# Rank columns beside the cross-attention queries, and the first up-projection begun in the output phases

## The reference

```python
for i in range(2):
    h = rms_norm(x, mix_norm[i])
    tok, xq = gla_mixer(h, ...) if i == 0 else dilated_mixer(h, ...)
    xa = memory_cross_attention(xq, mem_n, xa_w_kv[i], ...)
    x = x + concatenate([tok, xa]) @ w_out
    x = x + conv_ffn(rms_norm(x, ffn_norm[i]), w_up, conv_w, conv_b, w_down)
# gla_mixer: q, k, v, glr, og, xq = split_cols(h @ w_in, [384, 384, 768, 16, 768, 256])
#   log_a = log_sigmoid(glr @ w_gate2 + b_gate) / 16; chunked_gla(q, k, v, log_a); rms_norm(o) * silu(og)
# conv_ffn: u = causal_dwconv(h @ w_up, conv_w, conv_b); gate, val = split(u); (silu(gate) * val) @ w_down
```

## Time and profile before

| | us |
|---|---|
| median of 3 runs (2761.82 to 2763.5) | 2762.37 |
| the profiled execution | 2763.15 |
| its span (first to last instruction) | 2761.4 |
| PE busy | 2632.4 |
| PEld busy | 2224.0 |
| DVE busy | 1323.3 |
| ACT busy | 862.5 |
| POOL busy | 190.9 |

### The profile page before, as it was taken

How to read it: one execution, slowest core, us unless ns; L and a number is a source line. 1 busy time by engine, 2 the same in 40 slices (tenths; PEclk the granted TensorE clock), 3 DMA queues, 4 the chain that set the end, 5 groups by cost and what they waited for, 6 DMA issues and landing times. The chain is left out here.

```text
span 2761.4 us, 33638 instructions
## 1 busy us (share of the span) xinstructions
PE 2632.4 (95%) x12612; PEld 2224.0 (81%) x12612; DVE 1323.3 (48%) x2372; ACT 862.5 (31%) x1802; POOL 190.9 (7%) x265
## 2 busy tenths in 40 slices
PE   7998989989999999998999999998889999999999
PEld 7995767868888888886888888787768888888887
DVE  4422445435454455447463572453645445445445
ACT  6424434322222222224334433334332222222221
POOL 1000012000000000001211021111000000000000
PEclk9998999999999999999999999999899999999999
DMA  4211002122111111111101101102412111111111
GB/s 143 92 54 28 19 27 77 46 59 63 49 50 49 46 52 47 46 46 70 61 31 69 36 31 46 48 30 81 150 63 61 47 46 46 59 48 50 49 38 61
DMA packets 159282, 152.81 MB, mean 55 GB/s; under 512 B 27593, under 2 KB 129721, under 8 KB 159161
## 3 DMA queue, kind: packets, MB, share of 16 engines
q1 hardware_dynamic: 155000, 151.20, 17.1%
q10 hardware_dynamic: 4160, 0.02, 0.1%
HBM read 134.37 MB, written 16.83 MB: 55 GB/s over the span
## 5 line engine op out<-in xcount | busy, mean ns | idle before, releaser
L359 PE MATMUL psum<-hT_hi,f_up_hi 128*128 128x512 f32 x1408 | 435.8, 391 | 14.7 <-DVE f_up_lo L240 14.7
L359 PE MATMUL psum<-hT_lo,f_up_hi 128*128 128x512 f32 x1408 | 435.3, 390 | 0.0
L359 PE MATMUL psum<-hT_hi,f_up_lo 128*128 128x512 f32 x1408 | 434.8, 390 | 0.0
L50 PE MATMUL psum<-w_hi,hT_hi 128*128 128x512 f32 (+2 forms) x960 | 355.0, 370 | 19.5 <-DVE w_lo L736 11.3
L240 DVE TENSOR_TENSOR f_up_lo<-raw,f_up_hi 128x1024 fp32r<-128x1024 f32 x88 | 107.6, 1225 | 506.2 <-ACT f_up_hi L182 506.2
L52 PE MATMUL psum<-w_hi,hT_lo 128*128 128x512 f32 (+2 forms) x960 | 349.8, 364 | 0.0
L51 PE MATMUL psum<-w_lo,hT_hi 128*128 128x512 f32 (+2 forms) x960 | 349.6, 364 | 0.0
L359 PEld LDWEIGHTS psum<-hT_hi,f_up_hi 128*128 128x128 f32 x1408 | 265.1, 189 | 70.5 <-DVE f_up_lo L240 15.5
L359 PEld LDWEIGHTS psum<-hT_lo,f_up_hi 128*128 128x128 f32 x1408 | 265.4, 188 | 55.4
L359 PEld LDWEIGHTS psum<-hT_hi,f_up_lo 128*128 128x128 f32 x1408 | 265.3, 188 | 55.4
L182 ACT ACTIVATE f_up_hi<-raw 128x1024 fp32r<-128x1024 f32 x88 | 93.1, 1060 | 634.2 <-PE psum L359 599.8
(11 more groups left out here) (260 smaller groups left out, 3636.6 us busy)
## 6 DMA issues: line engine op xcount, KB each, us to landing
raw<-in_ffn_w_up_dram SPq DMA_DIRECT2D x88, 512.0 KB, 3.8
f_down_raw<-in_ffn_w_down_dram SPq DMA_DIRECT2D x22, 1024.0 KB, 4.8
w_raw<-in_b_w_in_dram SPq DMA_DIRECT2D x18, 1024.0 KB, 5.6
w_raw<-in_a_w_in_dram SPq DMA_DIRECT2D x8, 768.0 KB, 5.5
group_out<-stage SPq DMA_DIRECT2D x24, 256.0 KB, 2.3
o_outs<-group_out SPq DMA_DIRECT2D x24, 256.0 KB, 3.4
XY<-in_x_dram SPq DMA_DIRECT2D x8, 512.0 KB, 10.4
w_raw<-in_xa_w_kv_dram SPq DMA_DIRECT2D x8, 512.0 KB, 3.6
```

Of the source, the lines that this page charges most:

```text
L50: nc.tensor.matmul(out, lhs_hi, rhs_hi, start=start, stop=False)
L359: mm = nc.tensor.matmul(psum[:, 2 * j + half, :], w[j][:, d, :], h[:, d, half * HALF:(half + 1) * HALF], start=first, stop=final)
```

## The change

1. The rank columns are no longer loaded by the guest and projected in the gated phase. The block of the cross-attention queries gets them as 16 further columns (`beside_w`): SP loads them with a transfer of their own behind each half of the weights, the split and the matmuls cover 272 columns for 256, and ACT copies them out of PSUM per tile into `rank_rows`. The block now stands ahead of the two gate blocks, so that the second gate block ends the phase. In the gated phase eight turns of 128 x 16 (`turn_rank`) bring the rank columns into rows; `high(0)`, `low(0)` and `project(0, 0)` are gone, and the semaphore counts shift by one.
2. The split buffers of the up-projection (`FirstUp`) are made before the output phase and kept into the feed-forward phase; `y_hi`, `y_lo` use them until they are free. In the last tile the output phase makes the split of units 0 and 1, and PE does the first half (512 tokens) of each (`up_half`) behind the last output matmuls and behind the last turns. The turns of tile 6, and its gain and split, move ahead of the second half of tile 7. The feed-forward phase does only the second half of these two units, and its waits for `up_split` count from unit 2; SP's loads of units 2 and 3 wait for nothing there.
3. The stage tiles of the second layer are placed from the other side of the memory.

The diff, cut to its core:

```diff
# ffn_phase
                         n = g * 4 + 2 * c + j
                         if is_first(g) and c == 0:
                             continue
-                        sp.wait_ge(up_split, n - 1)
+                        if not is_first(g):
+                            sp.wait_ge(up_split, n - 3)
                         raws.load(sp, j, up_unit(w_up, j, g * 2 + c))
...
-                sp.wait_ge(up_split, 2 * FC)
+                sp.wait_ge(up_split, 2 * FC - 2)
...
-            high_up(0, 0)
-            high_up(1, 1)
             act.wait_ge(taps_ready, 1)
...
-            low_up(0, 0)
-            low_up(1, 1)
             dve.wait_ge(taps_turned, 1)
...
-                        pe.wait_ge(up_split, n + 1)
-                        if not is_first(g) or c:
+                        begun = is_first(g) and c == 0
+                        if not begun:
+                            pe.wait_ge(up_split, n - 1)
                             pe.wait_ge(conv_done, n - 1)
                         for d in range(DC):
                             for w, h, first, final in ((up_hi, hT_hi, d == 0, False), (up_hi, hT_lo, False, False),
                                                        (up_lo, hT_hi, False, d == DC - 1)):
-                                for half in range(2):
+                                for half in range(1 if begun else 0, 2):
# class FirstUp, out_phase
+class FirstUp:
...
+    def __init__(self, nc, ctx, ph):
+        def sb(name):
+            return ctx.enter_context(nc.sbuf_tensor(f"{ph}_{name}", [P, DC, P], F32R))
+        self.hi, self.lo = [sb(f"up_hi{j}") for j in range(2)], [sb(f"up_lo{j}") for j in range(2)]
...
+        y_hi = [x[:, 0:chunks, :] for x in up.hi]
+        y_lo = [x[:, 0:chunks, :] for x in up.lo]
+        up_raw = [x[:, :].rearrange("p (d n) -> p d n", d=DC) for x in raws.tiles]
+        up_loaded = [n + 16 for n in raws.count]
+        up_high, up_split = sem("up_high"), sem("up_split")
...
+            def high_up(j):
+                act.wait_ge(raws.loaded[j], up_loaded[j])
+                act.wait_ge(summed, 2 * (TT - 2 + j) + 2)
+                nc.scalar.activation(up.hi[j][:, :, :], up_raw[j], ACT.Copy).then_inc(up_high, 1)
...
             for t in range(TT):
                 if t + 1 < TT:
                     y_part(t + 1)
+                else:
+                    high_up(0)
+                    norm.act_high(act, t - 1)
                 act.wait_ge(x_ready, 2 * t + 2)
                 norm.act_square(act, t, XY[:, t, :])
+                if t == TT - 1:
+                    high_up(1)
                 norm.act_scale(act, t, XY[:, t, :])
-                if t >= 1:
+                if 1 <= t < TT - 1:
                     norm.act_high(act, t - 1)
             norm.act_high(act, TT - 1)
...
+            def low_up(j):
+                dve.wait_ge(up_high, j + 1)
+                nc.vector.tensor_tensor(up.lo[j][:, :, :], up_raw[j], up.hi[j][:, :, :].bitcast(F32), ALU.subtract).then_inc(up_split, 1)
             for t in range(TT):
                 dve.wait_ge(x_loaded, 16 * (t + 1))
                 for half in range(2):
                     if half and t + 1 < TT:
                         y_part(t + 1)
+                    elif half:
+                        norm.dve_gain(dve, t - 1)
+                        norm.dve_low(dve, t - 1)
                     cols = slice(half * HALF, (half + 1) * HALF)
                     dve.wait_ge(summed, 2 * t + half + 1)
                     nc.vector.tensor_tensor(XY[:, t, cols], psum[:, 2 * (t % 2) + half, :], x_old[:, cols], ALU.add).then_inc(x_ready, 1)
                 if merge and t + 2 < TT:
                     merge.dve_add(dve, t + 2)
-                if t >= 1:
+                if 1 <= t < TT - 1:
                     norm.dve_gain(dve, t - 1)
                     norm.dve_low(dve, t - 1)
+                if t == TT - 2:
+                    low_up(0)
+            low_up(1)
             norm.dve_gain(dve, TT - 1)
             norm.dve_low(dve, TT - 1)
...
+            def up_half(j):
+                pe.wait_ge(up_split, j + 1)
+                pe.wait_ge(x_ready, 2 * (TT - 2 + j) + 1)
+                for d in range(DC):
+                    split_matmul(nc, psum[:, 2 * j, :], up.hi[j][:, d, :], up.lo[j][:, d, :],
+                                 out_hi[:, d, 0:HALF], out_lo[:, d, 0:HALF], d == 0, d == DC - 1)
...
                         last = split_matmul(nc, psum[:, 2 * (t % 2) + half, :], y_hi[t % 2][:, k, :], y_lo[t % 2][:, k, :],
                                             w_hi[:, k, cols], w_lo[:, k, cols], k == 0, k == chunks - 1)
                     last.then_inc(summed, 1)
-                if t >= 1:
+                    if t == TT - 1 and half == 0:
+                        norm.pe(pe, t - 1)
+                if 1 <= t < TT - 1:
                     norm.pe(pe, t - 1)
+            pe.wait_ge(norm.low, HALF // P)
+            up_half(0)
             norm.pe(pe, TT - 1)
+            up_half(1)
# WeightSlots, project_phase
+    def load_beside(self, sp, s, w, n):
+        sp.dma_start(self.raw[s % 2][:, :, n:n + w.shape[1]], half_rows(w, s % 2)).then_inc(self.beside[s % 2], 16)
...
+        raw, hi, _ = self.parts(s, w, extra)
         self.wait_loaded(act, s)
+        if extra:
+            act.wait_ge(self.beside[s % 2], 16)
         self.nc.scalar.activation(hi, raw, ACT.Copy).then_inc(self.high, 1)
...
+                    slots.load_beside(sp, s, blocks[s // 2]["beside_w"], weights[s // 2].shape[1])
...
                         act.wait_ge(rows_ready, H - 1)
+                    if extras[b]:
+                        nc.scalar.activation(blk["beside"](t), psum[:, bank_of(b, t), n:n + extras[b]], ACT.Copy)
...
-                n = blk["w"].shape[1]
+                n = blk["w"].shape[1] + extras[b]
# gla_phase, Rope
-                    sp.wait_ge(w_split, h + 1)
+                    sp.wait_ge(w_split, h)
...
-                if s:
-                    act.wait_ge(w_loaded, 32 * s)
+                act.wait_ge(w_loaded, 32 * s)
+                if s >= 2:
                     act.wait_ge(projected, 2 * s - 1)
...
-            high(0)
             act.wait_ge(projected, 1)
...
+            def turn_rank():
+                for t in range(TT):
+                    turn = nc.tensor.transpose(psum[0:GLA_RANK, t // 4, t % 4 * P:(t % 4 + 1) * P], rank_rows[:, t, :], ident[:, :])
+                turn.then_inc(projected, 1)
...
-            project(0, 0)
+            turn_rank()
             pe.wait_ge(rank_ready, 2)
...
             sp.dma_start(dram.rearrange("p (t k) -> p t k", t=TT), self.tables[i]).then_inc(self.stored, 16)
         sp.wait_ge(self.stored, 16 * 2)
-        sp.dma_start(*self.last_load).then_inc(self.stored, 16)
-        sp.wait_ge(self.stored, 16 * 3)
# build
+                blocks += [dict(whole, kind="heads", dim=XA_DIM, gain=xa_gain[0][0][:, :], w=w[:, g0 + D_MIX:g0 + D_MIX + D_XA],
+                                pick=plain, dest=xa_dest(xqT), beside_w=w[:, g0 - GLA_RANK:g0], beside=lambda t: rank_rows[:, t, :])]
                 blocks += [dict(whole, kind="gate", w=w[:, g0 + i * B:g0 + (i + 1) * B], pick=plain, gain=o_gain[:, :],
                                 dest=lambda t, i=i: XY[:, t, i * B:(i + 1) * B]) for i in range(2)]
-                blocks += [dict(whole, kind="heads", dim=XA_DIM, gain=xa_gain[0][0][:, :], w=w[:, g0 + D_MIX:g0 + D_MIX + D_XA],
-                                pick=plain, dest=xa_dest(xqT))]
```

More of the change, by code:

```diff
@@ L90, in ffn_phase @@
         up_raw = [x[:, :].rearrange("p (d n) -> p d n", d=DC) for x in raws.tiles]
-        up_hi = [sb(f"up_hi{j}", [P, DC, P], F32R) for j in range(2)]
-        up_lo = [sb(f"up_lo{j}", [P, DC, P], F32R) for j in range(2)]
+        up_hi, up_lo = up.hi, up.lo
         down_raw = sb("down_raw", [P, 2, D])
@@ L701, in __init__ @@
         self.split = phase_semaphore(nc, ctx, f"{name}_split")
+        self.beside = [phase_semaphore(nc, ctx, f"{name}_beside{i}") for i in range(2)]
         self.base = 0
@@ L806, in project_phase @@
         weights = [b["w"] for b in blocks]
+        extras = [b["beside_w"].shape[1] if "beside_w" in b else 0 for b in blocks]
         extra_loaded, saved = sem("extra_loaded"), sem("saved")
@@ L945, in split @@
             def split(s):
-                slots.low_part(dve, s, weights[s // 2])
+                slots.low_part(dve, s, weights[s // 2], extras[s // 2])
             def tile(b, t):
@@ L1482, in _ @@
             dve.wait_ge(kept, 2)
-            low(0)
             low(1)
@@ L1523, in project @@
                         for half in range(2):
-                            mm = nc.tensor.matmul(psum[0:m, 2 * part + half, :], w[:, d, part * DK:part * DK + m],
+                            mm = nc.tensor.matmul(psum[0:DK, 2 * part + half, :], w[:, d, part * DK:(part + 1) * DK],
                                                   h[:, d, half * HALF:(half + 1) * HALF], start=first, stop=final)
```

(6 more changed lines are left out.)

65 lines of the change are left out of this document (30 added, 35 removed).

## The result

The changed kernel takes 2729.4 us in the median of four runs (2726.97 to 2731.02) against 2762.1 of four runs of the kernel before (2761.81 to 2763.5): a ratio of 0.988, 95% interval 0.9863 to 0.9897. Forecast were 2725.0, with a range of 2717 to 2738. Two further sets, each on a chip of its own, gave 2729.02 against 2762.03 and 2728.45 against 2762.12. The profiled execution took 2726.97 (span 2725.2), where the sum of the prediction made 2725.75. So in the profile 36.2 us went for 37.4 forecast; in the medians of the three sets 32.7 to 33.7.

A forecast was written before the change was run, and what follows sets the result against it. TensorE, busy 95% of the span, was taken as the bound, with waits at three phase hand-overs to win. Gains 1.8 + 11.5 + 12.3 + 11.8 = 37.4 us left 2725.75 profiled, 2725.0 in the median; range 2717 to 2738.

The forecast's parts named there:

- Part 1: Opening phase, cross-attention block moved ahead with 272 columns: 3.5 - 1.3 - 0.4 = 1.8 us gained.
- the 3.5 of the tail: End of the opening phase: a gate block's 1.1 us tail replaces the queries' 4.6 us, gaining 3.5.
- Part 2: Gated phase without rank weight split and projection: 11.85 + 1.7 - 2.0 = 11.5 us gained.
- The chain: Gated phase start: weight load, high part, low part, then the q/k projection starts 8.75 us in, against 20.6 before.
- The low stretch: Gated phase: one stretch at the low clock after the change, costing 0 to 2.65 us, taken as 2.0.
- Part 3: Output phase into feed-forward, half units filling TensorE's waits: 12.3 us gained in the first layer, 11.8 in the second.
- the stall of 0.4 for the convolution: Feed-forward start: unit 2 waits 0.4 us for the first unit's convolution, in each layer.
- the 0.65 that was to come back: Second layer's output phase: TensorE waits 0.65 us after the first half unit for the scaling of tile 7.
- A: Rival: clock falls in the new pause between output and feed-forward phase, 2.6 us a layer, 2730, at worst 2733; chance 0.18.
- B: Rival: unit 0's low part comes late, half units do not fill the wait; 6.8 us a layer, 2739; chance 0.08.
- C: Rival: 272 columns fall off the single-pass rate in the 192 matmuls, 77 us more, 2800; chance 0.03.
- D: Added loads or convolution chain stall more than counted, 1 to 3 us in three places, 2725 to 2734; forecast with D 0.68.

The follow-up runs named there:

- the rank part: Kernel before with only the rank columns beside the cross-attention queries and the gate blocks behind them, nothing of the up-projection: 2749.95 us.
- the up part alone: Kernel before with only the first halves of the first two up-projection units begun in the output phases, nothing of the rank columns: 2740.8 us.

## Why the prediction was right

**The bound and the places: right.** The gain is at the three hand-overs named, 1.95 + 12.35 and 11.8 and 11.3 us in the first profile. That these add up to 37.4, the forecast, is luck: the 12.35 hold 1.8 of low clock that fell well inside the gated phase, and 1.2 are lost again before the second output phase, which leaves 36.2.

**Part 1, 1.8 forecast, 1.95 measured: right term by term.** The width cost 0.1255 a matmul, 1.1 for 1.3. TensorE's last matmul of the phase starts 1.46 later (215.41 for 213.95), which is those 1.06 and the 0.4 of the turns. The phase's last work is done 1.46 after it (VectorE) for 4.9 before (ScalarE's copy), the 3.5 of the tail. The further loads cost nothing that shows.

**Part 2, 11.5 forecast; 10.5 to 11.1 up to the copy of the first projection, in three profiles.** The chain was right, its length 9.16 for 8.75: the weights landed at 5.75 for 5.4, and the low part ran to 9.1. The low stretch cost all of 2.65 where I took 2.0, since TensorE is at the full clock only from 235 on (window of after):

```profile
218.00:235.00 17.00, 10.87 (x25) 5.35 (x26) 1.90 (x2) 9.67 (x12) 1.07 (x2) 0.50 0.38 94
```

These two sizes are what was wrong in this part. Beyond the phase's start, other low stretches move the part by -1.8 to +1.3 from one execution to the next; I had counted the one at 243 and none of those behind it.

**Part 3, 12.3 and 11.8 forecast; 11.8 in all profiles and 11.3, or 9.7 to 9.8 where the clock fell.** The half units fill the waits, no split is late, the raw weights come at 6.7. Three sizes were off. The hand-over takes 1.75 and 2.18 where I took 1.5 for both: the row shows 1.61 (565.83 to 567.44) with 15 semaphores, the change added two in each layer, and the second layer has six more. The second half unit lasts 0.26 longer, as the phase ends with the end of its last matmul and not at the pace. And the stall of 0.4 for the convolution was 0.15 in the first layer and nothing in the second. In the second layer one wait was wrong altogether, PE and DVE of after:

```profile
1997.31 0.39 PE L50 MATMUL psum<-hT_hi,f_up_hi 128*128 128x512 f32 x1
...
2002.89 1.09 PE L453 MATMUL psum<-ident,o_scaled_rows 128*128 128x128 f32 x8
```

```profile
1998.86 0.68 DVE L669 TENSOR_TENSOR XY<-psum,o_x_old 128x512 f32<-128x512 f32 x1
```

VectorE takes up the last addition 1.55 us after the half unit's start, for 2.7 reckoned, so the turns follow after 5.57 and the 0.65 that was to come back does not. That made up for most of the 0.7 of the hand-over, by luck: two wrong terms nearly cancel in the 11.3. Behind the pause of 2.18 the clock sometimes falls, for 1.6 us.

**The rivals.** A happened, in part and in some executions: in one of three profiles of the changed kernel and in two of the seven with this pause, in the second layer only, at 1.6 us for 2.6. B did not: the low part of unit 0 is done at 538.19, 5.2 us before TensorE takes it up. C is refuted by the pace. D came to 0.4 in the gated phase and, at the feed-forward starts, to less than counted. Of the signs named beforehand two were missed by little: the projection starts 9.16 us into its phase for 8 to 9, and the second pause is 2.18 for under 2. The Trainium skill, TensorE: Matmul & The Clock Gate, "Why this matters for your kernels", warns of idle gaps between bursts of matmuls. The trace agrees for the gaps of 4.13 and 4.55 us; the 2.18 are shorter than the gaps that the page warns of and cost the clock in two of seven profiles all the same, and there the measurement decides.

**The sum.** 37.4 forecast, 36.2, 34.8 and 32.3 in three profiles, 32.7 to 33.7 in the medians. Of the difference 1.05 are in the gated phase's start (chain 0.4, low stretch 0.65) and 1.0 to 1.1 in part 3 (the hand-overs 0.25 and 0.7 longer; the second half units 0.26 each; the four half units in the feed-forward phases 0.17 each, since the first two matmuls behind other work start 0.31 apart for 0.227; the output phases' last matmuls 0.25 later in all; less 0.65 of stalls and some 0.6 by the wait that did not come). Another 0.5 stand at a hand-over that the forecast left out, inside the second layer's attention, in before and in after:

```profile
1892.49 0.82 PE L1101 MATMUL psum<-dil_kT,dil_qT 128*128 128x128 f32 x2 [2.64 <-PEq L2141]
```

```profile
1867.06 0.58 PE L1156 MATMUL psum<-dil_kT,dil_qT 128*128 128x128 f32 x1 [3.15 <-PEq L2192]
```

It comes with the rank part (3.09 alone; 2.64 with the up part alone): the second layer's weight slots have the two semaphores of the further loads too, without using them, and they are cleared there. That explains 0.14 of the 0.5; the rest is not explained. With 0.15 gained in part 1 the sum comes to 35.0. What is left, from 1.2 more to 2.7 less, goes with stretches at the low clock that fall differently in every execution, 1.6 of it with the fall behind the second pause. Which stretch contributes how often stays open: it would take many more profiles.

## What to carry to other kernels

A wait of the bounding engine at the end of a phase is filled best with the part of the next phase's work whose inputs are already there; two pieces did more than one, since the second hid the last split and kept the clock. When the waits are gone, read the pause that is put down to the sequencer: it was bookkeeping, 0.067 us for each semaphore and 0.33 for a barrier, and moving the clears under other work and leaving out the second barrier gave more than half as much as the whole change (18.5 us). A change that adds semaphores pays for them at the hand-over. Judge a term of 1 to 3 us by the distance of two instructions close to the edit, in more than one profile, not by medians that the clock spreads over 4 us.

## What the runs showed of the hardware

- Clearing a semaphore on GpSimd added 0.066 to 0.067 us to a hand-over (1.12 us for 17, 1.55 for 23; the clears start 0.071 apart); one barrier of all engines 0.33 us.
- The same instructions with the same pause of 2.18 us on TensorE left the clock at 1.00 in five profiles and at 0.50 in two; 1.75 left it up in seven of seven, and 4.13 and 4.55 lost it in the one profile that had them.
- The two plain float32 matmuls of the gate (four rows in the trace) took 3.72 us at the low clock and 1.95 at the full one.
- Matmuls in the rounded float32 type ran at 0.1255 us for 272 columns, on the line of 256 (0.120) and 384 (0.173).
